# Differential attention of a transformer block, its 32 row blocks taken in pairs of a short and a long one

## The reference, cut to what matters

```python
def block(i):                                   # 128 query rows
    sc = jnp.einsum('bhcqd,bhckd->bhcqk', qb, kt) * scale
    sc = jnp.where(mask, sc, -jnp.inf)          # causal
    p = jax.nn.softmax(sc, axis=-1)
    a = p[:, :, 0] - lam * p[:, :, 1]
    return jnp.einsum('bhqk,bhkv->bhqv', a, vt)
...
attn = rms_norm_2(attn, subln_w[l]) * (1.0 - lambda_init)
...
x = x + jnp.concatenate([attn, y], axis=-1) @ w_out[l]
```

## Time and profile before

| | us |
|---|---|
| median of 3 runs | 3368.28 (3362.66 to 3372.04) |
| profiled execution | 3378.69 |
| its span in the profile | 3376.9 |
| stage of the attention in it | about 2358 to 2611 |
| PE busy over the span | 3081.1 (91%) |
| DVE busy | 2033.2 (60%) |
| ACT busy | 1423.8 (42%) |

### The profile page before, as it was taken

The page is one execution under the profiler, slowest core; times in us unless marked ns, Lnnn a source line. Parts: engine busy times, 40 slices in busy tenths (PEclk is TensorE's granted clock), DMA queues, the critical chain, the costliest instruction groups (busy, mean ns, idle before and its releaser), DMA issues. The chain is left out here.

```text
span 3376.9 us, 59649 instructions
## 1 busy us (share of the span) xinstructions
PE 3081.1 (91%) x25098; PEld 2556.1 (76%) x25098; DVE 2033.2 (60%) x2955; ACT 1423.8 (42%) x2147; POOL 458.4 (14%) x349
## 2 busy tenths in 40 slices
PE   8999999688887999797999999998777799999999
PEld 5878887677776889576999977777555688888887
DVE  6746446577675613453555534754454788888887
ACT  4434433233333323473444432542454554554443
POOL 0122221121122122200000022211101000000000
PEclk9999999799897999998999999999898899999999
DMA  8432232432214212324111023112300222221953
GB/s 303 142 131 96 76 122 105 106 72 66 66 35 169 82 44 75 121 107 152 57 54 62 29 86 116 52 60 99 120 30 14 99 78 85 82 88 69 311 162 125
DMA packets 204840, 333.16 MB, mean 99 GB/s; under 512 B 73760, under 2 KB 137376, under 8 KB 201120
## 3 DMA queue, kind: packets, MB, share of 16 engines
q1 hardware_dynamic: 181248, 244.56, 22.0%
q0 software_dynamic: 22464, 84.42, 7.2%
q10 hardware_dynamic: 864, 0.38, 0.0%
HBM read 238.48 MB, written 90.83 MB: 98 GB/s over the span
## 5 line engine op out<-in xcount | busy, mean ns | idle before, releaser
L60 PE MATMUL ev_ps<-h_hi,even_ring_hi 128*128 128x512 f32 (+1 forms) x792 | 288.1, 364 | 1.3 <-DVE late_area L808 1.3
L60 PE MATMUL ff_ps<-ff_op,ff_w_hi 128*128 128x512 f32 x672 | 263.8, 393 | 21.2 <-DVE ff_w_lo L3615 18.3
L62 PE MATMUL ev_ps<-h_hi,even_ring_lo 128*128 128x512 f32 (+1 forms) x792 | 280.5, 354 | 0.0
L61 PE MATMUL ev_ps<-h_lo,even_ring_hi 128*128 128x512 f32 (+1 forms) x792 | 280.5, 354 | 0.0
L61 PE MATMUL ff_ps<-ff_op,ff_w_hi 128*128 128x512 f32 x672 | 263.0, 391 | 0.0
L62 PE MATMUL ff_ps<-ff_op,ff_w_lo 128*128 128x512 f32 x672 | 262.8, 391 | 0.0
L60 PEld LDWEIGHTS ev_ps<-h_hi,even_ring_hi 128*128 128x128 f32 x792 | 149.6, 189 | 39.8 <-issue 19.6
L3182 ACT ACTIVATE ma_e<-ma_s,ma_nm 128x1280 f32<-128x1280 f32 x64 | 84.9, 1327 | 216.4 <-DVE ma_nm L3218 216.4
L61 PEld LDWEIGHTS ev_ps<-h_lo,even_ring_hi 128*128 128x128 f32 x792 | 149.8, 189 | 21.7 <-issue 1.7
L62 PEld LDWEIGHTS ev_ps<-h_hi,even_ring_lo 128*128 128x128 f32 x792 | 149.6, 189 | 21.2
L60 PEld LDWEIGHTS ff_ps<-ff_op,ff_w_hi 128*128 128x128 f32 x672 | 127.0, 189 | 48.8 <-DVE ff_w_lo L3615 22.0
(11 more groups left out here) (582 smaller groups left out, 8298.1 us busy)
## 6 DMA issues: line engine op xcount, KB each, us to landing
w_up_raw<-in_w_up SPq DMA_DIRECT2D x48, 512.0 KB, 4.4
w_up_raw<-in_w_down SPq DMA_DIRECT2D x34, 512.0 KB, 5.0
even_ring_raw<-in_ev_w_in POOLq DMA_DIRECT2D x33, 512.0 KB, 3.8
late_area<-in_ada_w SPq DMA_DIRECT2D x32, 512.0 KB, 5.2
ffn_mid<-h POOLq DMA_DIRECT2D x24, 512.0 KB, 2.9
ff_mem<-ffn_mid SPq DMA_DIRECT2D x24, 512.0 KB, 11.1
ar<-late_area SPq DMA_DIRECT2D x8, 1280.0 KB, 5.2
bk<-late_area SPq DMA_DIRECT2D x8, 1280.0 KB, 7.2
```

The source lines that it names most:

```text
L60: nc.tensor.matmul(out, w_hi, x_hi, start=start, stop=False, skip_group_check=resumed)
L61: nc.tensor.matmul(out, w_hi, x_lo, start=False, stop=False, skip_group_check=resumed)
L62: return nc.tensor.matmul(out, w_lo, x_hi, start=False, stop=stop, skip_group_check=resumed)
```

## The change

The order of a head becomes qt = 0, 7, 1, 6, 2, 5, 3, 4: even units are short, odd ones long, and the loops count pairs of a short and a long unit, 16 of them, with up to 22 steps. The short unit of a pair is 2s, the long one 2s+1. There is a fill in each of the steps 1 to 16, so still 16 in all, and it stands after both scores. The short score of step s waits for the add of step s-1. The number of instructions on each engine is the same, and so are their shapes.

```diff
-    SEQ = [(h, qt) for h in range(NH) for qt in (7, 0, 6, 1, 5, 2, 4, 3)]
+    SEQ = [(h, qt) for h in range(NH) for qt in (0, 7, 1, 6, 2, 5, 3, 4)]
...
-                    if fill_of(u - 1) is not None:
-                        pe.wait_ge(added, fill_of(u - 1) + 1)
+                    if u % 2 == 0 and u >= 4:
+                        pe.wait_ge(added, u // 2 - 1)
...
+                for s in range(LAST_STEP):
+                    old = 2 <= s < PAIRS + 2
+                    if s < PAIRS:
+                        score(2 * s)
+                    if 3 <= s < PAIRS + 3:
+                        values(2 * s - 5)
+                    if old:
+                        turn(2 * s - 4, 0)
+                    if s < PAIRS:
+                        score(2 * s + 1)
+                    if old:
+                        turn(2 * s - 3, 0)
+                    if has_fill(s):
+                        fill(s)
+                    if old:
+                        values(2 * s - 4)
+                        turn(2 * s - 3, 1)
+                    if s >= 7 and s % 4 == 3:
+                        head_sums(s // 4 - 1, 0)
+                        head_sums(s // 4 - 1, 1)
...
+                    new, old = s < PAIRS, 2 <= s < PAIRS + 2
+                    if new:
+                        exponentials(2 * s)
+                    if old:
+                        turned_out(2 * s - 4, 0)
+                    if 1 <= s < PAIRS + 1:
+                        first_part(2 * s - 2)
+                        first_part(2 * s - 1)
+                    if old:
+                        turned_out(2 * s - 3, 0)
+                    if new:
+                        exponentials(2 * s + 1)
+                    if old:
+                        turned_out(2 * s - 3, 1)
+                    if s >= 7 and s % 4 == 3:
+                        squares(s // 4 - 1)
+                        head_roots(s // 4 - 1)
...
+                    new, late = s < PAIRS, 1 <= s < PAIRS + 1
+                    if new:
+                        maximum(2 * s)
+                    if late:
+                        factors(2 * s - 1)
+                    if 3 <= s < PAIRS + 3:
+                        store(2 * s - 5)
+                    if late:
+                        difference(2 * s - 2)
+                    if new:
+                        maximum(2 * s + 1)
+                        factors(2 * s)
+                    if late:
+                        difference(2 * s - 1)
+                    if has_fill(s):
+                        add(s - 1)
+                    if 2 <= s < PAIRS + 2:
+                        store(2 * s - 4)
+                    if s >= 8 and s % 4 == 0:
+                        normalize(s // 4 - 2)
```

More of the change, by code:

```diff
@@ L2083, in phase_diff_attention @@
     NH, NQ = 4, LAT // P
-    SEQ = [(h, qt) for h in range(NH) for qt in (7, 0, 6, 1, 5, 2, 4, 3)]
+    SEQ = [(h, qt) for h in range(NH) for qt in (0, 7, 1, 6, 2, 5, 3, 4)]
     N = len(SEQ)
+    PAIRS = N // 2
+    LAST_STEP = PAIRS + 6
     tiles_of = lambda u: SEQ[u][1] + 1
@@ L2088, in phase_diff_attention @@
     CUM = [sum(len(chunks(v)) for v in range(u)) for u in range(N + 1)]
-    NE, NP, LAST = 3, 3, N + 6
+    NE, NP = 3, 3
     HALF = KD // 2
@@ L2093, in phase_diff_attention @@
     filled, added = g.sem("da_filled"), g.sem("da_added")
-    fill_of = lambda s: (s - 2) // 2 if s % 2 == 0 and 0 <= (s - 2) // 2 < FILL else None
+    has_fill = lambda s: 1 <= s <= FILL
     mask_in, lam_prod, lam_dots, lam_exp, lam_diff, lam_out, weight_done = (
@@ L2147, in _ @@
                     nc.gpsimd.tensor_tensor(lo[:, 4 + c], yin[c], hi[:, 4 + c].bitcast(F32), ALU.subtract).then_inc(y_lo, 1)
[L2148 to L2151, removed]
+                for j in range(1, NH + 1):
+                    low_of_tile(nc, pool, ring, a0 + j)
+                    load_tile(pool, ring, a0 + j + 1)
+                    if j >= 2:
+                        low_part(j - 2)
+                low_part(NH - 1)
             @block.tensor
@@ L2198, in fill @@
                 def fill(s):
-                    f = fill_of(s)
+                    f = s - 1
                     m, o = f // 2, BANK * (f % 2)
@@ L2204, in fill @@
                         pe.wait_ge(ring.lo_done, a0 + f // 4 + 1)
-                    pe.wait_ge(exps, 2 * min(s, N))
+                    pe.wait_ge(exps, 2 * min(2 * s + 1, N))
+                    if f:
+                        pe.wait_ge(added, f)
                     t = (a0 + f // 4) % 2
@@ L2224, in _ @@
                 pe.wait_ge(lam_exp, 1)
[L2225 to L2234, removed]
-                        fill(s)
[L2236 to L2240, removed]
+                for s in range(LAST_STEP):
[11 more added lines that the diff above has]
+                    if has_fill(s):
+                        fill(s)
+                    if old:
[4 more added lines that the diff above has]
+                        head_sums(s // 4 - 1, 1)
             @block.scalar
@@ L2303, in _ @@
                 split_tile(1)
[L2304 to L2322, removed]
+                for s in range(LAST_STEP):
+                    new, old = s < PAIRS, 2 <= s < PAIRS + 2
[15 more added lines that the diff above has]
+                        head_roots(s // 4 - 1)
+                    if s >= 9 and s % 4 == 1:
+                        high_part(s // 4 - 2)
+                    if s in (6, 10, 14):
+                        split_tile((s - 6) // 4 + 2)
             @block.vector
```

2 lines of the change are left out of this document (1 added, 1 removed).

## The result

| | before | after |
|---|---|---|
| median, us | 3370.16 (4 runs) | **3331.28** (4 runs, 3328.57 to 3335.08) |
| ratio of after to before | | 0.9885, 95% interval 0.9871 to 0.9898 |
| span of the profiled execution | 3376.9 | 3326.8 |
| stage, from the product for lambda to the next stage's first product | 252.3 (2359.1 to 2611.4) | 205.1 (2356.4 to 2561.5) |
| first score to last store | 230.6 | 184.5 |

The change makes the kernel 39 us faster. The forecast was 3321 in a range of 3308 to 3343, so the range holds the time and the likeliest value was 10 us too low. The two profiled executions alone differ by 47.2 us in this stage, exactly the gain that was forecast; the difference between 47 and 39 is part of what the experiments had to explain.

A forecast was written before the change was run, and what follows sets the result against it. No engine is full; a chain through several bounds the stage, PE waiting 30.8 us for ACT's copies and 11.0 ahead of short scores. 179 us against 230.6 gains 51, less 4 is 47: from median 3368.3 to 3321, range 3308 to 3343.

The forecast's parts named there:

- From S to E: From PE's end of a pair's short score to its end of the long score: 30.8 us of copy waits go.
- From E to the next short score: From PE's end of the long score to the next pair: 4.5, 4.6, 4.5 and 4.4 us, set mainly by DVE's chain.
- The second copy's cover: ACT's copy behind the long exponentials is ready 0.4 to 1.2 us before PE wants it for values.
- The sums: At a head's end, squares stand behind the last copy, costing 4 us more for each of three heads.
- On POOL the low parts move: POOL's low parts move behind the next weight tile; POOL busy 22 of 222 us, so no effect on time.
- Ends and sum: First steps, steady steps and draining add up to 179 us from first score to last store, against 230.6 before.
- the 4 us that I took off for wakings: Subtracted from the 51 us gain, a quarter microsecond a pair, for PE reaching semaphores just around their release.
- The clock, 10 us: Seven long scores in the steady part, slowed by clock dips, take about 10 us more than their sizes ask.
- Dips stay: Rival: remaining short waits still cause clock dips on PE, so 10 us do not come back: 3331 us; chance 0.14.
- Copies late: Rival: long exponentials come 1 us later, PE waits for values in most pairs, 16 to 25 us back: about 3341; chance 0.11.
- No gain: Rival: a DVE and ACT ring already takes 13 us a pair, so time stays within 10 us of 3368; chance 0.04.
- slower: Rival: short difference, long maximum, exponentials, second copy and values form a ring through three engines, for example 3389 us; chance 0.05.

The follow-up runs named there:

- a_values_first: The changed kernel with PE doing the values of the older long unit ahead of the short score instead of behind it; 3345.44 us, ratio to before 0.9940.
- a_copy_behind: The changed kernel with ACT's first copy of a long unit's turned tiles put back behind the long exponentials; 3351.67 us, ratio to before 0.9949.
- a_diff_behind: The changed kernel with DVE's short difference behind the long maximum instead of ahead of it; 3332.32 us, ratio to before 0.9899.
- b_copy_first: The kernel before, unpaired, with two ACT lines exchanged so the first turned tiles are copied ahead of the exponentials; 3340.33 us, ratio 0.9913.

## Why the prediction came out as it did

**What bounds the kernel: right.** PE's wait for copies stood ahead of everything, and the exchange of two lines that touches nothing but their place took 30 of the 43 us; putting it back cost 22 to 24, some 5 of them clock.

**PE's work per head, 36.8 us at full clock: right.** Eight tiles take 2.47 us up to the next piece (2405.40 to 2407.87), forecast 2.46. In the steady stretch after has no long score at the lower level.

**From S to E: nearly right.** "The 30.8 us go, bar remainders of some tenths": 2.4 us remain. The part of a seven-tile pair from its start to E is 5.30 us (2412.33 to 2417.63) where 9.7 - 4.6 = 5.1 stood.

**From E to the next short score: right to 0.2 us.** Forecast 4.5, 4.6 and 4.5 for b = 8, 7 and 6, measured 4.46, 4.59 and 4.32 in the first head. The pairs took 9.88, 9.89 and 9.08, forecast 9.7, 9.7 and 9.1.

**The second copy's cover, 0.4 to 1.2 us: right.** 0.8 us of waits in all, and a_values_first shows what stands on the other side of it: 12.8 us of waits for the second copy and a stage 16 us longer.

**The sums, 4 us a head: right, a little low.** E + 5.76 and E + 8.72 against 5.6 and 8.4; the fourth pair takes 14.39 us, forecast 9.8 + 4 = 13.8.

**"On POOL the low parts move ...; so nothing": the step that failed.** I asked whether POOL is free and whether its result is late, not whom it holds while it works. Two of POOL's products overlap a negation in later heads and stretch it to 0.7 to 0.9 us, on the path to the short exponentials: in the second and third head the six-tile pair takes 9.85 us instead of 9.08. The sum of after had no term for this. The hold isn't new with the change: before's own trace has a wait of 2.75 us behind a held negation where 0.94 stood without it, and the prediction counted it among the 30.8 us of waits put down to ACT's order. With the negation out of the way, and the squares and the tile's split moved, the stage became another 10 us shorter. The Trainium skill, "SBUF — State Buffer", section "Who interferes with whom", states this: GpSimd and some forms on VectorE share one pair of ports as an exclusive lock; whoever issues first has it for its whole instruction and the other is blocked meanwhile, while on this chip a reduction never contends. The rows agree, with the 2.18 us negation behind a 2.34 us product and the reduction that ran through one undisturbed.

**Ends and sum.** Measured, with the forecast in brackets: steps 0 and 1 19.1 us (20.5), step 2 9.1 (9.0), step 3 9.95 (9.8), steps 4 to 15 43.2 + 44.0 + 44.0 = 131.2 (127), drain 15.1 (13). The sum is 184.5 against 179, or 183 with the 4 us that I took off for wakings. So most of the 4 us were needed, for other reasons than the one given: POOL's holds in two heads 1.5, the drain 2.1, the sums 0.6 in each of three heads, the pairs' starts about 1 in all; steps 0 and 1 gave 1.4 back.

**The clock, 10 us: right in this trace, too high as a rule.** It is what the first trace of before held; the other two held 8 and 5, and in the third more waiting for copies took part of the difference back. The step that failed is the passage from one trace to the median: the prediction carried the whole gain of one execution over and only shifted its base by 10.4 us. That execution of before was the longest of three in the stage and the one of after not the longest, so 4.2 of the 10 us between 3321 and 3331 are 47.2 against a mean of 43.0. Another 1.9 are the base (3370.2 against 3368.3). The last 2 to 4 are medians that gain 41.3 and 38.9 where the stage gains 43.0; with 13 us of scatter outside the stage between single traces no run here says where they are, and that stays open.

**Rivals.** *Dips stay* gives 3331, the number measured, and isn't the cause: in the first two traces of after the clock in the steady stretch is 1.00, and its waits of 0.2 to 1.6 us are followed by full-speed work. It isn't empty either. Behind such waits around a head's sums the third trace of after lost 1.6 us to the clock, and that of a_copy_behind 5.6; in before a seven-tile score took 3.48 us instead of 2.25 behind a wait of 0.94. The Trainium skill, "TensorE: Matmul & The Clock Gate", section "A second HAM failure mode: psum-queue depth-cycling", was cited for this rival: its swings between the two levels are seen in these places and not as a rule. *Copies late* is what a_values_first looks like. *No gain* and *slower* are refuted; a_diff_behind shows that moving the difference behind the maximum gains nothing.

**Signs.** Stage 47 us shorter: 47.2 in that trace, 43 in the mean. Waits for copies gone from the top: yes. PE over 90% busy at a clock of 0.97 or more: 92% at 1.00. Eight-tile score 2.5: 2.47. One gap around the sums in each head but the last: yes, 4.4 us (8.72 - 4.32) where 4 was forecast.

## What to carry to other kernels

Where the engine that bounds a kernel waits for a small step (a copy out of a single bank) queued behind a large one on another engine, try the exchange of these two lines first: here it gave 30 of 43 us, and the rebuilt order (the pairs, with POOL's work placed elsewhere) gave the rest. When an instruction moves in time, ask not only who waits for it but whom it holds while it runs; a two-number instruction on the critical path is worth folding into its neighbour for that reason. Sum a forecast over one trace, but price what scatters between executions (clock, chance overlaps) at its mean and not at what that one trace holds.

## What the hardware showed that I had not expected

- A VectorE multiplication of two numbers a row (0.17 us) took 0.69 to 2.35 us when it starts behind a 2.34 us GpSimd product on 128 x 1024 elements, and ends within some hundredths of a microsecond of it; a product of one number a row took 1.02 us in the same way. A reduction from PSUM, started behind such a product too, was not slowed. Whether the small instruction comes 0.05 us ahead of GpSimd or 0.18 behind it made 2.2 us of difference between two executions of one kernel.
- The granted clock answers to waits between products in an uneven way: behind waits of 2.60 us a long score ran at full speed or mostly at half, in the same kernel and stage. With waits of 0.8 to 0.9 us at every fill (b_copy_first, 11.1 us in all) the stretch ran at 1.00, but behind waits of 1.10, 1.52 and 0.78 us (a_copy_behind) it fell to 0.53 in one head and not in the next.
- Removing a wait can pay twice: in the exchange of two lines the waits for copies fell by 24 us and the stage by 30; slow long scores had cost 5 to 10 us and were gone. That they went because the waits went is argued from this, not shown by a run of its own.
